# A two-layer decoder trunk on eight cores: block order, convolution buffers and the gathering of states

## The reference

```
h = rmsnorm(x); u, q, k, v, b, c, h2 = split(h @ w_in)      # 256, 3 x 384, 3 x 384 channels
y_pool = pool_mix(u)                 # causal window means over 2, 4, 8, 16 tokens, minus u, times pool_w
y_attn = attention(q, k, v)          # 3 dilation groups of 2 heads, QK-norm, rotary, merged by denominators
y_conv = b * conv3(c * h2)           # causal width-3 convolution per channel
x = x + concat(y_pool, y_attn, y_conv) @ w_out
x = x + square(relu(rmsnorm(x) @ w_up)) @ w_down             # 4096 hidden channels
```

## Time and profile before

| | |
|---|---|
| median of three runs | 1432.34 us (1430.84 to 1433.47) |
| the profiled execution, its own time | 1430.84 us |
| its span, slowest core (core 6) | 1429.3 us (cores: 1418.1 to 1429.3) |
| TensorE busy | 1380.4 us (97%), 8921 matmuls |
| VectorE, ScalarE, GpSimd busy | 821.7, 705.7, 385.1 us |
| chain that ended last | 89% TensorE, 4% DMA |
| read from and written to HBM | 159.63 MB, 47.90 MB |

### The profile page before, as it was taken

How to read it: one execution, slowest core, us unless ns; L and a number is a source line. 1 busy time by engine, 2 the same in 40 slices (tenths; PEclk the granted TensorE clock), 3 DMA queues, 4 the chain that set the end, 5 groups by cost and what they waited for, 6 DMA issues and landing times.

```text
span 1429.3 us, 28093 instructions; the slowest of 8 cores (1418.1 to 1429.3 us)
## 1 busy us (share of the span) xinstructions
PE 1380.4 (97%) x8921; PEld 787.5 (55%) x8921; DVE 821.7 (57%) x1534; ACT 705.7 (49%) x1495; POOL 385.1 (27%) x561
## 2 busy tenths in 40 slices
PE   6999998899999999999999999899999999999998
PEld 2555665455555555555555566555555555555554
DVE  1878876774444444446677788867644444444443
ACT  3657665664244342436646566557444343433522
POOL 4566747340000000002236666653000000000000
PEclk8999999999999999999999999999999999999999
DMA  9851447960652490143245052399037228200122
GB/s 202 204 83 33 89 107 166 230 89 1 120 77 77 92 180 1 19 85 95 73 98 126 26 88 55 95 261 164 3 82 114 77 64 133 76 1 1 49 97 96
DMA packets 81679, 133.33 MB, mean 93 GB/s; under 512 B 14008, under 2 KB 70520, under 8 KB 81152
## 3 DMA queue, kind: packets, MB, share of 16 engines
q0 software_dynamic: 53952, 79.29, 30.4%
q1 hardware_dynamic: 18880, 49.10, 11.6%
q10 hardware_dynamic: 8704, 3.15, 0.9%
HBM read 159.63 MB, written 47.90 MB: 145 GB/s over the span
## 4 chain that ended last, share of the span: by engine, by line
PE 89%; DMA 4%; issue 2%; POOL 2%; DVE 1%; ACT 1%; SPq 0%; DVEq 0%; POOLq 0%; ACTq 0%
PE psum L1767 32%; PE psum L1743 31%; PE psum L1357 9%; PE psum L1172 9%; PE psum L1720 4%; DMA big<-xin 1%; PE psum L1589 1%; DMA big<-xin_r 1%; POOL big L859 1%; DMA big<-xpark 1%; PE psum L1480 1%; DMA kv_p<-big 1%; PE psum L1003 1%; PE psum L1564 0%; PE psum L1614 0%
## 5 line engine op out<-in xcount | busy, mean ns | idle before, releaser
L1743 PE MATMUL psum<-big 128*128 128x416 bf16 x2560 | 457.6, 339 | 2.3 <-DVE big L1755 1.5
L1767 PE MATMUL psum<-big 128*128 128x416 bf16 x2560 | 456.6, 339 | 0.0
L1743 PEld LDWEIGHTS psum<-big 128*128 128x128 bf16 x2560 | 249.2, 98 | 202.7 <-issue 6.2
L1767 PEld LDWEIGHTS psum<-big 128*128 128x128 bf16 x2560 | 249.8, 98 | 199.8 <-issue 1.7
L1758 ACT ACTIVATE big<-big 128x416 f32<-128x416 f32 x291 | 159.6, 549 | 403.8 <-DVE big L1755 402.9
L1755 DVE TENSOR_TENSOR big<-psum,big 128x416 f32<-128x416 f32 x320 | 188.8, 591 | 231.5 <-PE psum L1743 173.5
L1770 DVE TENSOR_TENSOR big<-psum,big 128x416 f32<-128x416 f32 x320 | 189.0, 591 | 226.7 <-PE psum L1767 226.1
L1759 ACT ACTIVATE big<-big 128x416 bf16<-128x416 f32 x320 | 175.0, 549 | 49.0 <-POOL big L1757 6.1
L1172 PE MATMUL psum<-big 128*128 128x416 bf16 x880 | 172.3, 345 | 5.5 <-ACT big L1093 1.4
L1357 PE MATMUL psum<-big 128*128 128x384 bf16 (+1 forms) x816 | 140.5, 326 | 2.3 <-ACT big L1576 2.3
L860 ACT ACTIVATE big<-big 128x416 bf16<-128x416 f32 (+5 forms) x139 | 87.3, 636 | 82.6 <-DVE big L1724 36.1
(11 more groups left out here) (144 smaller groups left out, 1155.2 us busy)
## 6 DMA issues: line engine op xcount, KB each, us to landing
big<-w_up POOLq DMA_DIRECT2D x32, 512.0 KB, 13.5
big<-w_down POOLq DMA_DIRECT2D x32, 512.0 KB, 10.5
kv_s<-c SPq DMA_DIRECT2D x8, 2040.0 KB, 12.4
big<-xin_r POOLq DMA_DIRECT2D x10, 832.0 KB, 8.7
xpark<-big SPq DMA_DIRECT2D x10, 832.0 KB, 4.1
big<-xpark POOLq DMA_DIRECT2D x10, 832.0 KB, 13.9
yout<-big SPq DMA_DIRECT2D x20, 416.0 KB, 2.4
big<-xin POOLq DMA_DIRECT2D x8, 832.0 KB, 13.0
```

What stands on the lines that cost most here:

```text
L1743: bi = yield late(1, lambda bi: pe([(BL, lambda e, d=d: e.matmul(bank(bi)[:, 0:BL], lhsT=WU[i][:, d, 128 * fc:128 * fc + 128], rhs=HT[:, d ...
L1767: bi = yield late(1, lambda bi: pe([(BL, lambda e, f=f: e.matmul(bank(bi)[:, 0:BL], lhsT=WD[i][:, f, 128 * oc:128 * oc + 128], rhs=AT[a][: ...
```

## The change

The new kernel differs in these parts:

- The blocks of the MLP come in the order 0, 1, 2, 3, 4 (in layer 0's last quarter 4, 3, 0, 1, 2 where it was 4, 0, 3, 1, 2). `PLACE` and `VN` are gone: outputs and norms lie by block number.
- `conv_item` has two buffers for the gate (`GCS`, held to the end of the h product) and two for the rest (`CACC`), in place of four that serve both.
- `store_hist` gathers both states in one piece, after the last block's convolution and pooling, and one event `hstored` releases both slots.
- The first quarter's `w_up` waits for all convolution and pooling outputs (`proj_done`).

```diff
-    PLACE = [0, 2, 1, 3, 4]
...
-    VN = [4, 1, 2, 3, 0]
...
-    CACC = [m([128, BL], F32, ("cacc", i)) for i in range(4)]
+    GCS = [m([128, BL], F32, ("gcs", i)) for i in range(2)]
+    CACC = [m([128, BL], F32, ("cacc", i)) for i in range(2)]
...
-        if l:
-            yield wait(*[ev("up", l - 1, 3, VN.index(b), fc) for fc in range(8)])
...
-        yield wait(ev("atts", l))
+        yield wait(ev("atts", l), *[ev("hs", l, x) for x in range(5)], *[ev("cz", l, NB - 1, cc) for cc in range(3)], *[ev("pw4", l, pc) for pc in range(2)])
...
-        K.spawn(part([ev("hs", l, x) for x in range(2)] + [ev("pw4", l, pc) for pc in range(2)], ev("hgp", l),
...
-        K.spawn(part([ev("hs", l, x) for x in range(2, 5)] + [ev("cz", l, NB - 1, cc) for cc in range(3)], ev("hgc", l),
...
+        K.fire(ev("hstored", l))
+        yield wait(ev("att", l, 3))
...
-        ci = yield acq(PCA)
-        ca, kc = CACC[ci], ("cacc", ci)
-        gs, kg = ca, kc
+        gi = yield acq(PGC)
+        gs, kg = GCS[gi], ("gcs", gi)
...
-        K.fire(ev("hm", l, b, cc))
+        K.release(PGC, gi)
+        ci = yield acq(PCA)
+        ca, kc = CACC[ci], ("cacc", ci)
...
-    ORDER = [[[0, 2, 1, 3, 4]] * 3 + [[4, 0, 3, 1, 2]], [[0, 2, 1, 3, 4]] * 4]
+    ORDER = [[list(range(NB))] * 3 + [[4, 3, 0, 1, 2]], [list(range(NB))] * 4]
...
-            yield wait(*[ev("om", l, x, oc) for x in range(NB) if PLACE[x] // 2 == k for oc in range(8)])
+            yield wait(*[ev("om", l, x, oc) for x in (2 * k, 2 * k + 1) for oc in range(8)])
...
-        done = {SC: conv_done + [ev("atts", l), ev("hgc", l)], SP_: pool_done + [ev("hgp", l)], SQ_: qk_done, ...
+        done = {SC: conv_done + [ev("atts", l), ev("hstored", l)], SP_: pool_done + [ev("hstored", l)], SQ_: qk_done, ...
...
-                wu, wd = [ev("hm", l, NB - 1, cc) for cc in range(3)] + [ev("ru", l, NB - 1, 3 + pc) for pc in range(2)], qk_done + ...
+                wu, wd = proj_done, qk_done + ...
```

More of the change, by code:

```diff
@@ L890, in build_program @@
     PSQR, PSQ, PQF, PQB, PS4, PPB, PROT = Pool(range(2)), Pool(range(2)), Pool(range(3)), Pool(range(2)), Pool(range(4)), Pool(range(1, NP)), Pool([0])
-    PCA, PPS, PCK, PSS, PNORM = Pool(range(4)), Pool(range(2)), Pool([0]), Pool(range(2)), Pool([0])
+    PGC, PCA, PPS, PCK, PSS, PNORM = Pool(range(2)), Pool(range(2)), Pool(range(2)), Pool([0]), Pool(range(2)), Pool([0])
     PVST = Pool(range(3))
@@ L1124, in norm2 @@
         K.fire(ev("n2", l, b))
-        v = VN[b]
-        yield wait(*[ev("om", l, x, oc) for x in ((0, 1), (2, 3), (4,), (4,), ())[v] for oc in range(8)], *r_free(l, v))
-        yield ops(act(BL, lambda e: e.activation(out=VB[v], in_=bank(bi)[:, 0:BL], func=AF.Ln, scale=1.0 / D, bias=EPSC[:, 0:1]), [("ps", bi), "epsc"], [kvb(v)], True))
+        yield wait(*[ev("om", l, x, oc) for x in ((0, 1), (2, 3), (4,), (4,), ())[b] for oc in range(8)], *r_free(l, b))
+        yield ops(act(BL, lambda e: e.activation(out=VB[b], in_=bank(bi)[:, 0:BL], func=AF.Ln, scale=1.0 / D, bias=EPSC[:, 0:1]), [("ps", bi), "epsc"], [kvb(b)], True))
         K.release(BANKS, bi)
-        yield ops(act(BL, lambda e: e.activation(out=VB[v], in_=VB[v], func=AF.Exp, scale=-0.5), [kvb(v)], [kvb(v)]))
+        yield ops(act(BL, lambda e: e.activation(out=VB[b], in_=VB[b], func=AF.Exp, scale=-0.5), [kvb(b)], [kvb(b)]))
         K.fire(ev("r2", l, b))
@@ L1212, in mix_free @@
         o = ORDER[l - 1][3]
-        return w + [ev("down", l - 1, 3, x) for x in (o[:-1] if PLACE[b] < 2 else o if b < 4 else [])]
+        return w + [ev("down", l - 1, 3, x) for x in (o[:-1] if b < 2 else o if b < 4 else [])]
     def pool_item(l, b, pc):
@@ L1753, in up @@
             rl, kr = SS[ri], ("ss", ri)
-        v = VN[b]
-        yield ops(dve(BL, lambda e: e.tensor_tensor(out=rl, in0=bank(bi)[:, 0:BL], in1=VB[v], op=ALU.mult), [("ps", bi), kvb(v)], [kr]))
+        yield ops(dve(BL, lambda e: e.tensor_tensor(out=rl, in0=bank(bi)[:, 0:BL], in1=VB[b], op=ALU.mult), [("ps", bi), kvb(b)], [kr]))
         K.release(BANKS, bi)
@@ L1877, in mlp @@
             if fb == 0:
-                wu, wd = [ev("hm", l, NB - 1, cc) for cc in range(3)] + [ev("ru", l, NB - 1, 3 + pc) for pc in range(2)], qk_done + [ev("vsh", l, 3, g, pr) for g in (1, 2) for pr in range(2)]
+                wu, wd = proj_done, qk_done + [ev("vsh", l, 3, g, pr) for g in (1, 2) for pr in range(2)]
             elif fb == 1:
```

17 lines of the change are left out of this document (6 added, 11 removed).

## The result

The changed kernel takes 1441.26 us (median of four runs, 1440.01 to 1445.02) against 1431.59 us of the kernel before in four runs beside it: a ratio of 1.0071, 95% interval 1.0047 to 1.0094, so 6.7 to 13.5 us slower. The profiled execution took 1440.14 us with a span of 1438.5 us on core 6, 9.2 us more than the span before on the same core.

The account below looks back on a forecast made before the run. TensorE was taken as the bound, so the price was its idle time in the mixers: layer 0 +4.3, clock +1.0, loads 0, buffers and order 0, together +5.3 us, so 1437.6 us at the median; range 1430.5 to 1443.

Parts of the forecast that it names:

- The filler goes: Layer 0: block 2's late reload puts all 40 out-projection groups, not 28, behind the last values; 8.5 us more there.
- The attention comes earlier: Layer 0: with less TensorE work ahead, the last values end at 244.2, 4.2 us earlier than before.
- rival A: Layer 0's attention profits more: values end at 235.1, 13.3 us earlier; kernel 1427.5 us; chance 0.14.
- my objection to A: Layer 0: block 2's first half lands only at 241.8, and VectorE cannot empty the out-projection's banks before.
- The clock: End of layer 0's attention: one more group at 1.2 GHz after TensorE waits; +1.0 us, bounds 0 and 2.
- The loads: Layer 0's first `w_up` loads move behind ten reloads, first load at 236; covered by the out-projection, cost nothing.
- Rival B: Late convolution product delays gathering; loads from 245 on reach `up` 3.2 us late; +8.5 us, 1440.8 us; chance 0.18.
- Two and two buffers: 0: Layer 1: ten projection groups move behind the last q, k, v product; bounds -4.6 and +5.3, middle 0 taken.
- the other reading: A distance arising before 200 us or in layer 1 would make the convolution's two buffers the cause, not the reload.
- C: No difference: layer 0's chain stays at 21.1 us without more idle time or clock loss; +1.1, 1433.4 us; chance 0.18.

Follow-up runs that it names:

- e3: Kernel before with one part alone: first `w_up` loads wait for all projections of the layer; ratio 0.9998.
- e2: Kernel before with one part alone: two and two convolution buffers in place of four shared ones; ratio 1.0015.
- e5: Changed kernel with the histories stored in two pieces again, each releasing its own slot; ratio 1.0072 to the kernel before.
- e11: Changed kernel with three shared convolution buffers in place of two and two; ratio 0.9993 to the kernel before.
- e6: Changed kernel with the four shared convolution buffers again; ratio 1.0058 to the kernel before.
- e1: Kernel before with one part alone: histories stored in one piece, one event releasing both slots; ratio 1.0128.
- e9: One-piece history alone on the kernel before, plus first `w_up` and `w_down` loads held behind the conv and pooling slots' reloads; ratio 0.9984.
- e10: Changed kernel with two-piece history, plus first `w_down` loads held behind all reloads of the layer; ratio 1.0072 to the kernel before.
- e7: Changed kernel with first `w_up` loads released again by the last convolution and pooling states; ratio 1.0116 to the kernel before.

## Why the prediction was right or wrong

The forecast of +5.3 us had the sign and half of the size (+9.7 by the medians). By the medians over the cores, layer 0 lost 7.0 us to the eleventh `up` group, where the forecast had 5.3 with the clock, and layer 1 another 3.2, where it had none. By its steps, on core 6:

- **The filler goes.** The row of 40 groups is there. From the end of the last values to the second `up` group it takes 288.18 + 1.41 - 239.07 = 50.5 us, predicted 45.7. The mis-sized term is the waits behind the values: taken 1.5, measured 4.06 + 0.66 = 4.7; the rest is the 1.7 us of lower clock. The 1.5 was a misreading of the earlier trace rows: it matches the last of three waits there, and the place that I took it from has 2.07 + 1.03 + 1.48 = 4.6 us, with which the sum would have been 3.1 us higher. I had let a reload take 2.5 us by its bytes, but five issued together deliver the first after 10.18.
- **The attention comes earlier.** The last q, k, v product starts at 220.88, predicted 221.3. The stretch to the end of the values takes 18.2 us, predicted 22.9 and 21.1 before; the 1.8 us that I added for VectorE's operations do not show. The values end at 239.07, outside the 242 to 246 I named and past rival A's point. Yet A did not happen: what the values gained, the missing residual took, as my objection to A said (block 2's half at 241.8; it was 245.6). Layer 0 to the second `up` group is 13.3 - 9.3 = +4.0 where I had +4.3: two errors of 5 us that cancel, so the agreement is luck and no proof of the working. The idle time between 200 and 290 us is 9.96, not 12 to 15.
- **The clock.** A stretch under 1.00 is at 246 to 252 us, worth 1.7 us, but from 50 us on layer 0 has two such stretches in each trace, at 55 and 194 us before (the earlier trace rows shows the second) and at 94 and 247 us after, so it gains none on this core. Two more lie in layer 1, where I had none.
- **The loads.** First load taken at 236, issued at 234.57; no `up` group waits for `w_up`. Rival B is wrong here, though e3 shows that its wait exists.
- **Two and two buffers: 0.** This step failed. Layer 1 loses 3.9 us on core 6, inside the bounds of -4.6 to +5.3; 3.4 of them are the two stretches of lower clock, but the medians over the cores, most of which have none there, still show 3.2. The waits behind the values did go, as the lower bound had it, and waits inside the attention came, which I had not listed; e2 shows them with the buffers alone.
- **The cause.** I named the reload that the one-piece history delays. The text's own sign for the other reading, a distance that arises in layer 1, appeared, and e5 and e11 decide which part the loss hangs on: undoing the history gives nothing back, replacing two and two by three removes the loss. Replacing them by the four of before leaves 8.3 us of it (e6), since the one piece then costs in layer 1. The history is dear where weight loads can slip ahead of the reloads (e1, e6; e9 takes it away); that no out-projection is left ahead of layer 0's last values takes a convolution that ends late as well (changed against e11). C is wrong: the lists do what they say.

What stays open is why two and two cost only 2 us alone and some 8 more with the later `w_up` loads and the history in either form (e2 against e5): e5 shows the reload wait in layer 0 as its place, and e10 takes that wait away but puts as much waiting into the MLP, so it neither confirms nor refutes this.

## What to carry to other kernels

Where one engine issues bulk loads and compute operands from one list, read what stands ahead of the operand that is needed first: holding 4 MB of weights behind it was worth some 20 us here (e1 against e9). Parts of a change that move filler are not additive, so undo each part in the changed kernel as well as trying it alone. When a sum comes out right, check the terms; here two of them were off by 5 us in opposite directions.

## What the runs showed of the hardware

- A store of k and v (issued in pairs of 128 KB) took 8.19 us in the chain with four weight loads issued around it (e1), 7.78 with four others (e6), 4.53 with none (e9); a reload of 832 KB took 10.18 us from issue to landing with one weight load ahead and five reloads issued together (changed), 14.92 and 15.11 with three and four weight loads ahead (e5, e7). The Trainium skill (DMA: Bandwidth & Descriptors, Queues, rings and completion order) has the DMA engines take turns between queues packet by packet; the store, on SyncE's queue, still nearly doubled.
- The stretches at a mean clock of 0.72, part 1.2 and part 2.4 GHz, lie at waits of TensorE as short as 1.0 us (with one of 0.58 us next to it) and 1.3 us, on a core that was otherwise busy; in layer 1 of the changed kernel cores 6 and 7 have two, core 2 one, and the other five none, with the same lists.
